# Wide products that nobody reads at three norm turns, and four modulation tiles moved into latent attention

## What is computed

```python
c_act = silu(c)
for i in range(2):
    mod = c_act @ mod_w[i] + mod_b[i]                 # 12288 columns, six parts of 2048
    sh_m, sc_m, g_m, sh_f, sc_f, g_f = split(mod, 6)
    h = modulate(rmsnorm(x, norm_mix_g[i]), sh_m, sc_m)
    y = gla_mixer(h) if i == 0 else mla_attention(h, shared_kv)   # shared_kv from x, own shift and scale
    x = x + (1 + g_m) * y
    h = modulate(rmsnorm(x, norm_ffn_g[i]), sh_f, sc_f)
    x = x + (1 + g_f) * conv_ffn(h)                   # up 2048 -> 2 x 5632, conv, silu gate, down
return rmsnorm(x, final_norm_g)
```

## Time and profile before

| | us |
|---|---|
| median of 3 runs | 2360.09 (2359.97 to 2363.09) |
| the profiled execution, its own time | 2362.72 |
| its span in the trace | 2360.1 |
| PE busy | 2295.1 (97%) |
| DVE busy | 1848.8 (78%) |
| ACT busy | 1095.5 (46%) |

### The profile page before, as it was taken

The page is one execution under the profiler, slowest core; times in us unless marked ns, Lnnn a source line. Parts: engine busy times, 40 slices in busy tenths (PEclk is TensorE's granted clock), DMA queues, the critical chain, the costliest instruction groups (busy, mean ns, idle before and its releaser), DMA issues.

```text
span 2360.1 us, 26865 instructions
## 1 busy us (share of the span) xinstructions
PE 2295.1 (97%) x10800; PEld 1869.5 (79%) x10800; DVE 1848.8 (78%) x1767; ACT 1095.5 (46%) x1192; POOL 113.5 (5%) x129
## 2 busy tenths in 40 slices
PE   5999999999999999999998989999999999999997
PEld 2478887788888888888887889888888888888886
DVE  5868997887998988888989878887787556565565
ACT  2234443444554354543554545444664445544453
POOL 0021740000000000000000000000000000000000
PEclk8999999999999999999999999999999999999999
DMA  9957789797987998889989466786776555555554
GB/s 362 386 195 287 250 297 361 270 330 265 351 319 293 346 349 309 296 327 362 328 286 336 128 223 213 295 311 224 275 285 214 196 184 190 178 196 194 181 185 153
DMA packets 259808, 632.89 MB, mean 268 GB/s; under 512 B 23506, under 2 KB 32746, under 8 KB 233979
## 3 DMA queue, kind: packets, MB, share of 16 engines
q1 hardware_dynamic: 258050, 625.90, 74.6%
q10 hardware_dynamic: 1656, 5.60, 0.6%
HBM read 629.36 MB, written 2.10 MB: 268 GB/s over the span
## 4 chain that ended last, share of the span: by engine, by line
PE 54%; issue 34%; DVE 6%; DMA 4%; ACT 1%; SPq 1%; POOL 0%; POOLq 0%; DVEq 0%; ACTq 0%
PE gm L1964 14%; PE gm L1965 14%; PE gm L1971 14%; PE tp L2007 2%; PE gm L1956 1%; PE gm L1958 1%; PE gm L1957 1%; DVE acc L1245 1%; DVE w_lo L1228 1%; DMA raw<-in_ffn_w_down_dram 1%; PE ms L2117 1%; DMA mods<-in_mod_w_dram 1%; PE ms L2251 1%; DVE acc L1480 1%; DMA raw<-in_gla_w_in_dram 1%
## 5 line engine op out<-in xcount | busy, mean ns | idle before, releaser
L1228 DVE TENSOR_TENSOR w_lo<-raw,w_hi 128x2048 fp32r<-128x2048 f32 (+1 forms) x378 | 851.7, 2255 | 317.6 <-ACT w_hi L766 316.0
L766 ACT ACTIVATE w_hi<-raw 128x2048 fp32r<-128x2048 f32 (+1 forms) x378 | 703.8, 1864 | 701.0 <-DMA raw<-in_ffn_w_up_dram 254.1
L1964 PE MATMUL gm<-w_hi,h_hi 128*128 128x512 f32 x1816 | 720.7, 397 | 1.6 <-DVE h_lo L1356 1.6
L1965 PE MATMUL gm<-w_hi,h_lo 128*128 128x512 f32 x1816 | 708.1, 390 | 0.0
L1971 PE MATMUL gm<-w_lo,h_hi 128*128 128x512 f32 x1816 | 448.7, 389 | 0.0
L1245 DVE SCALAR_TENSOR_TENSOR acc<-mods,c_col,acc 128x2048 f32<-128x2048 f32 x180 | 422.6, 2348 | 5.7 <-DMA mods<-in_mod_w_dram 4.4
L1964 PEld LDWEIGHTS gm<-w_hi,h_hi 128*128 128x128 f32 x1816 | 341.2, 188 | 78.2 <-issue 6.0
L1971 PEld LDWEIGHTS gm<-w_lo,h_hi 128*128 128x128 f32 x1816 | 340.8, 188 | 70.8
L1965 PEld LDWEIGHTS gm<-w_hi,h_lo 128*128 128x128 f32 x1816 | 341.3, 188 | 69.9 <-issue 1.7
L1964 PE MATMUL gm<-w_hi,a_hi 128*128 128x512 f32 x692 | 273.8, 396 | 2.9 <-ACT w_hi L766 2.8
L1965 PE MATMUL gm<-w_hi,a_lo 128*128 128x512 f32 x692 | 269.6, 390 | 0.0
(11 more groups left out here) (277 smaller groups left out, 2146.9 us busy)
## 6 DMA issues: line engine op xcount, KB each, us to landing
raw<-in_ffn_w_up_dram SPq DMA_DIRECT2D x176, 1024.0 KB, 5.1
mods<-in_mod_w_dram SPq DMA_DIRECT2D x170, 1024.0 KB, 7.1
raw<-in_ffn_w_down_dram SPq DMA_DIRECT2D x64, 1024.0 KB, 5.1
raw<-in_gla_w_in_dram SPq DMA_DIRECT2D x48, 1024.0 KB, 5.2
mods<-in_kv_mod_w_dram SPq DMA_DIRECT2D x32, 1024.0 KB, 7.1
raw<-in_ffn_w_down_dram SPq DMA_DIRECT2D x32, 768.0 KB, 4.3
raw<-in_gla_w_o_dram SPq DMA_DIRECT2D x16, 1024.0 KB, 6.9
raw<-in_mla_w_o_dram SPq DMA_DIRECT2D x16, 1024.0 KB, 5.5
```

The costliest lines, as they stand in the source:

```text
L766: act.activation(w_hi[:, k % RAW, 0:words], raw[:, k % RAW, 0:words], ACT.Copy).then_inc(hi_made, 1)
L1228: dve.tensor_tensor(w_lo[:, k % RAW, 0:words], raw[:, k % RAW, 0:words], w_hi[:, k % RAW, 0:words].bitcast(F32), ALU.subtract).then_inc(lo ...
L1964: pe.matmul(o, hi_s[:, kt, tok], wh[:, j, :], start=kt == 0, stop=False)
L1965: pe.matmul(o, lo_s[:, kt, tok], wh[:, j, :], start=False, stop=False)
```

## The change

Three edits. (1) Four tiles of group 11 leave items 10 to 13 of down02 and go to items 6, 9, 12 and 15 of mla; the number in latent_out's wait follows from the table (the tiles of group 11 that stand ahead of the latent section, 6 before and 2 now; they share memory with lat). (2) In the reduce of groups 4, 10 and 12, a product 352 columns wide stands ahead of the one-column products 4, 8 and 12. It multiplies two constant tensors in float32 and writes to gm, which the next item overwrites; nobody reads it. Ahead of the reduce PE asks that gm's half be free. (3) One more such product stands after the first two fills of transposes and ahead of the wait for the first split.

```diff
-            ("down02", 10, 12, every[4:8]), ("down02", 11, 0, (8, 9, 10, 11, 12, 13)),
-            ("mla", 11, 6, (2, 3, 4, 5, 7, 8, 10, 11, 13, 14)),
+            ("down02", 10, 12, every[4:8]), ("down02", 11, 0, (8, 9)),
+            ("mla", 11, 2, every[2:]),
...
-                    act.wait_ge(mod_used, 8 * KT + 22)
+                    act.wait_ge(mod_used, 8 * KT + 18)
...
-            def reduce_mod(g, parts=range(4)):
+            def keep_busy(count):
+
+                for _ in range(count):
+                    pe.matmul(gm[:, 0, 0, 0:4 * 2 * FT], ones[:, :], cv_col[:, 0].rearrange("p a b -> p (a b)"),
+                              start=True, stop=True)
+
+            def reduce_mod(g, parts=range(4), busy_from=None):
...
                     o = ms_open(fill)
+                    if busy_from is not None:
+                        gm_free(busy_from)
                     for j in range(KT):
+                        if busy_from is not None and j in (4, 8, 12):
+                            keep_busy(1)
                         ins = pe.matmul(o[:, j:j + 1], acc[:, g % 2, j * P:(j + 1) * P], ones[:, 0:1],
                                         start=True, stop=True)
...
                     if name in BOUND:
+                        keep_busy(1)
                         pe.wait_ge(first_lo, BOUND[name] + 1)
                         return
...
-            reduce_mod(4)
+            reduce_mod(4, busy_from=a["up00"].chunk)
...
-            reduce_mod(10)
+            reduce_mod(10, busy_from=a["latent"].chunk)
...
-            reduce_mod(12)
+            reduce_mod(12, busy_from=a["up10"].chunk)
```

## The result

The changed kernel takes 2348.49 us (median of 6 runs, 2345.68 to 2354.89); the kernel before 2360.03 (median of 6, 2359.7 to 2363.09). The ratio is 0.9947, 95% interval 0.9938 to 0.9957: 11.5 us faster, where 14.2 were forecast. The execution that was profiled is the fastest of the six (span 2343.8), and the profiled one before is 2.7 us above its median, so the two profiles show more gain than the medians do.

The account below looks back on a forecast made before the run. It took PE, busy 97% of the span, as the bound, with time to win only where it waits or runs slow. -9.6 + 0.5 - 5.1 = -14.2 us gave 2345.9 us in medians (chance 0.48), range 2343.0 to 2355.5.

Parts of the forecast that it names:

- the first rival: At the three turns the clock falls as before, so the products cost 2.0 us and win nothing: 2353.0 us, chance 0.37.
- Rival 2: down02 stays bound by its loads, items 12 to 14 remain late, gain there only 7.8 us: 2347.7 us, chance 0.10.
- part 1: Four tiles out of down02: waits before its late items and the last item's half clock go, gain 9.6 us (8.8 to 10.5).
- Part 2: Four tiles put into latent attention: DVE's lag delays PE's head steps, cost 0.5 us, bounds 0 and 9.0.
- DVE just keeps up, but can't catch up any more: In latent attention with a tile in each step, DVE takes 14.99 us for two steps, PE 15.06 for two items.
- Rival 3: VectorE becomes the bound in latent attention, with PE waits and half clocks: slower, 2368.1 us, chance 0.05.
- Part 3: Wide products at norm1, norm2 and norm5 keep the clock at 1.00: 5.1 us gained over three turns.
- Does it stay?: Clock at the turns: longest stretch without a wide product, 2.2 us, lies between idle waits of 1.70 and 2.53; leaned to holding.
- the reduce's length: At the turns, three wide products add 1.77 us to a reduce of 4.12, making 5.89 from the last item's end.
- The other term: First item behind a turn: 2.2 us of its half clock go and no more, since DVE's chain doesn't get shorter.

Follow-up runs that it names:

- the six-tile run: Changed kernel with the tiles of items 8 and 9 of down02 also moved, as second tiles in latent attention's steps 7 and 12: 2353.77 us, ratio 0.9967.
- one block: Changed kernel with each reduce's three wide products together ahead of column 8, not one each ahead of columns 4, 8 and 12: ratio 0.9941.
- The variant with 512 columns: Changed kernel with the three wide products of each reduce 512 columns wide in place of 352: 2350.05 us, ratio 0.9958.

## Why the prediction was right, and where it wasn't

11.5 us came against 14.2; 14.2 and 12.1 came by medians when the same kernel was run again. 2348.49 lies in the range of 2343.0 to 2355.5 and between the forecast (2345.9) and the first rival (2353.0). Rival 2 named 2347.7, nearer still, but its mechanism isn't what happened, as part 1 shows: that is a coincidence of the number.

**Part 1** was right in mechanism and somewhat high in size. 9.6 us were forecast; the stretch from up00 to the end of down02 gives 9.4 in the changed kernel's profile and 10.4 with the tiles alone, but over all ten profiles that have these four tiles moved and no others it is 751.0 to 755.4 us, against 761.05 and 761.45 with the tiles in place: 8.6 on average, from 5.9 to 10.2. The least gain is that of the profile with the convolution's waits and the half clock behind them. The 3.74 us wait and the half clock behind it went together in all ten. The wait before item 12, of which I left 0.85, was in fact 0.7 to 1.8 us, 1.3 on average. I had taken its raw load as unchanged, and it was: 9.25 us in the changed kernel, and 9.2 from its issue until ACT has it before (the load behind the 9.98 of the earlier trace rows is that of a later item). The first row is the changed kernel's chain of waits, the other two SP's issue of the load and ACT's rounding before the change:

```profile
1256.43 9.25 DMA raw<-in_ffn_w_down_dram
1262.56 0.43 SPq L548 DMA_DIRECT2D raw<-in_ffn_w_down_dram  x1
1271.83 1.48 ACT L766 ACTIVATE w_hi<-raw 128x1536 fp32r<-128x1536 f32 x1 [3.94 <-DMA raw<-in_ffn_w_down_dram]
```

Rival 2 took that remainder as it was but expected items 13 to 15 late as well; no profile shows that.

**Part 2**, +0.5 us with bounds 0 and 9.0: at like clock behind the wait of mla_out, the profiles with the four tiles have 280.35 to 281.07 us, and those without them 280.35 and 281.24. So about nothing. "DVE just keeps up, but can't catch up any more" was the right reading, and the six-tile run shows that the room ends there. The idle time that DVE shows there is its wait of 0.73 us for the exponential in each pair of steps. Rival 3 was nearer than its 0.05: with two more tiles its lag appeared, though at 6.4 us and not with the half clocks that it added.

**Part 3** is where the forecast failed, in its step "Does it stay?". I took the longest stretch without a wide product, 2.2 us, to decide, and let it stand between two idle waits. At norm2 the clock fell inside the reduce, where PE is 100% busy and no such stretch is over 1.0 us; one block with 1.7 us of bare columns kept it in three turns. So the quantity was wrong, and with it the assumption that the three turns go the same way: 13 of 24 kept the clock. Forecast and rival 1 are not two outcomes of the kernel but two outcomes of each turn, with a third between them, a half clock of only 3.4 us. What decides in one execution which of them comes stays open.

The prices of a turn were also off, in both directions. By how the clock went, the 24 turns compare with those of the two profiles without products like this: where it was kept (13 turns) a turn is 2.4 us shorter on average (1.6 to 2.9), where I had 2.1 and 1.5; at half clock for 3.4 us (5 turns) it is 1.6 us shorter; for 6.8 us (6 turns) 0.2 us longer, from 0.5 shorter to 1.5 longer (the longest has a wait of 2.0 us for xn besides), where rival 1 had 0.5 to 1 longer. The step that put the kept turns too low is the reduce's length. I added three products to 4.12 us, but the clock had fallen 3.0 us into that reduce, so part of the 4.12 was at half clock. At full clock the 16 columns take 3.2 us and the three products 2.0 (1.77 forecast), so the transposes start 5.26 us after the reduce's start and not 5.89. At norm5 faster transposes then give back what the products cost (first product 7.57 us after the reduce's start, before 7.56), where I had 0.7 lost; at norm1 it comes 0.65 us earlier (7.57 against 8.22), where I had it 0.1 later. The other term held: from there to the fifth K tile PE takes 6.76 us (528.39 to 535.15) in place of 8.83, 2.1 less for 2.2 forecast.

Over the 24 turns a turn is 1.58 us shorter, 4.7 for three, and 4.8 is what the products alone gave. That is near the forecast 5.1 by luck: the kept turns gained more than I said, and the six with the longer half clock gained nothing.

The Trainium skill, "TensorE: Matmul & The Clock Gate", section "Part 4: PE-mode transpose", says that transposes don't count as a busy PE in the way that products do, and I weighed it as speaking for the first rival. For most of the falls the transposes can't be the reason. In the kernel before, the clock fell 2.5 to 3.0 us after the reduce's start and the transposes began 4.8 to 5.5 us after it; in the changed kernel's turns 9 of the 11 falls come before the first transpose. How the chip counts a transpose is shown by no run here.

**The sum by what was measured**: -8.6 (part 1, ten profiles), 0 (part 2), -4.7 (part 3, eight profiles) is -13.3, or 2346.8 us; the medians were 2348.49, 2347.51 and 2348.8 with a spread of 4 to 13 us, so up to 2 us stay open. The turns before and after are not of the same executions, and the start of the kernel alone moves by over 4 us between profiles.

## What to carry to other kernels

Where TensorE is busy with one-column products and transposes between two stretches of wide ones, look at the granted clock of the item behind them, not only at the waits: here it was 10 us at half speed three times. Wide products in waits that are there anyway cost the least; those that lengthen the path have to be paid by the clock that they keep. Judge such a change by the turns of several profiles and by the time of many executions: one profile here showed anything from no turn at half clock to all three. And before work is moved onto an engine that keeps pace by 0.07 us in 15, count how many pieces its idle time holds: four tiles cost nothing here, two more cost 6.4 us.

## What the runs showed of the hardware

- The granted clock fell with PE 100% busy on products of one column, in the reduce and not behind it (1287.5 us in the changed kernel; 2.5 to 3.0 us after the reduce's start at each turn of the kernel before), and with the wide products the same program lost it at other turns in each execution, for 3.4 or 6.8 us in place of 10.2.
- A wait of 2.5 to 2.7 us in mla_out, at the same place in eleven profiles, was followed by half clock in eight of them and not in three: idle time of that length alone doesn't decide it.
- Between one-column products a float32 product of 352 columns takes 0.67 us at full clock (521.63 to 522.30).
- The variant with 512 columns had three turns at full clock in its profile and still ran from 2345.4 to 2356.9 us. One execution took 2349.89 us at a mean clock of 0.994, another 2345.37 at 0.993: a part of the spread between executions isn't TensorE's clock. What it is stays open.
